# Sample tile's output projection moved into score banks and cut into quarters around the first memory tile

## Chip, cores, metric

One Trainium2 chip, one core. The time is the device time of one execution in microseconds (us), lower is better; several runs are taken and the median is given.

## What is computed (the reference, cut)

One layer of a streaming encoder for 512 prompt tokens and 64 sample tokens of width 1024. After the mixers (gated linear attention, pooling, differential attention) comes their output projection, then cross-attention to 256 memory tokens, then a mixture of 16 experts:

```python
mix = concatenate([o_gla, o_pool, o_diff.reshape(B, L, DIFF_V)], axis=-1)   # 256 + 256 + 512 columns
x = x + mix @ w_out
h = rmsnorm(x, norm_mem_g)
q = (h @ w_mem_q).reshape(B, L, MEM_HEADS, MEM_DH)                          # 4 heads of 128
s = einsum('bqhd,bkhd->bhqk', q, mk) * MEM_DH ** -0.5
p = softmax(s, axis=-1)
x = x + einsum('bqhk,bkhd->bqhd', p, mv).reshape(B, L, 512) @ w_mem_o
x = x + hier_moe(rmsnorm(x, norm_ffn_g), ...)                               # top-1 group, top-2 experts in it
```

Everything is float32. The kernel gets that precision from fast matmuls by splitting each operand into a rounded part ("high", float32r) and the rest ("low") and summing three products: high x high, high x low, low x high.

## The kernel before

**Tiles.** The tokens are five tiles: t = 0 to 3 with 128 prompt rows each, t = 4 with the 64 sample rows. For t = 4 high and low rows stand side by side in one 128-column operand, so a projection of that tile takes two matmuls for each block of 128 inputs, where the others take three; DVE then adds the two halves of the result.

**Who does what.** PE (TensorE) multiplies and transposes, ACT (ScalarE) rounds weights and transposed activations to their high parts and takes exponentials, DVE (VectorE) subtracts to get the low parts, adds projections to the residual `xw`, copies and normalises. POOL does the reciprocal roots of the norms, SP issues the loads of weights. Each engine has one written list of instructions, in order; engines wait for each other by counting semaphores.

**Banks.** PSUM has eight banks of 512 columns: `pj0`, `pj1` for projections, `tr_v`, `tr_a` for transposes, four for scores (`sc`), used in two halves of 1024 columns in turn. Three plans written by hand at the top (`projection_plan`, `transpose_plan`, `score_plan`) list every use of a bank in order, who reads it ("A" for ACT, "V" for DVE) and which bank it takes. `claim` in PE's program makes PE wait until the last user of the same bank has been read out. `high_plan` lists ACT's rounded transposes, which DVE's `low_T` waits for.

**Dense weights.** `w_in`, `w_out`, `w_mem_q`, `w_mem_o` come as 24 units of 128 x 2048, through four slots (`DRING`). Unit n takes the slot of unit n - 4, and may be loaded (SP, `dense_load`) or, for the memory query units 20 and 21, which have buffers of their own, rounded (ACT, `w_high`) when the last projection that uses unit n - 4 is done. Units 16 and 17 serve columns 0 to 511 of the mixers' projection, `w_out(0, t)`; 18 and 19 serve `w_out(1, t)`; 20 and 21 (`MQ_UNIT`) the memory queries; 22 and 23 (`MO_UNIT`) the memory output. So `w_out(0, 4)` releases 20 and 21, and `w_out(1, 4)` releases the loads of 22 and 23. `mem_q(0)` waits for DVE's `w_low` quarter by quarter (L2189), since it is the first user.

**The order around the change.** Twenty attention steps (tile, head) end with the differential attention of the sample tile. Beside its last step runs the last quarter of `w_out(1, 3)`. Then the sample's heads are normalised: ACT squares, DVE sums, POOL takes roots (L770), DVE multiplies twice into `mixd`. After that PE's list is:

```python
mixd_T(TILES - 1)          # transposes of the sample's normalised heads, bank tr_v
x1_T(0)                    # transposes of residual tile 0, halves g = 1 (tr_a), 0 (tr_v)
w_out(0, TILES - 1, 0); w_out(0, TILES - 1, 1)     # 16 matmuls, bank pj1
w_out(1, TILES - 1)                                # 16 matmuls, bank pj0
x1_T(1)
mem_q(0); mem_q_T(0); mem_scores(0)                # 24 matmuls (pj1), 4 transposes (tr_v), 8 matmuls
```

`mixd`, `mgT_pack`, `plT_pack` are the inputs of `w_out(c, 4)`: only its second half (blocks 4 to 7) needs `mixd`. Then five memory tiles follow. In tile t PE does `mem_q(t + 1)`, the transposes of the probabilities `probm` (`pm`, one half in `tr_a` for ACT, one in `tr_v` for DVE, copied at L1873), `w_mem_o(0, t - 1)`, the transposes of query t + 1 (`mem_q_T`, bank `tr_v`, copied by DVE at L1839), the memory output `mem_o(t)`, the transposes `x1_T(t + 2)`, `mem_scores(t + 1)` and `w_mem_o(1, t - 1)`. ACT evacuates `mem_q` to `rowbuf` (L985) and takes the exponentials (`exps_m`, L1279). ACT rounds units 22 and 23 before the exponentials of tile 0. DVE splits unit 22 after the row maxima of tile 0, unit 23 after those of tile 1. The first expert weights are loaded when `mem_q(4)` is done.

Lines in the profile: L2167 is the matmul helper `mm`, L2175 the transposes, L967 and L970 `w_high`, L1479 and L1450 the low parts (L1450 is any two-operand DVE operation), L944 ACT's high parts of transposes, L563 the load of units.

Of the kernel before, what the change touches and what calls it, by code (L numbers as in the profile page):

```python
# [10 lines left out]
ALU = mybir.AluOpType  # L11
# [68 lines left out]
def projection_plan():  # L80
# [11 lines left out]
    plan += [(("w_out", c, TILES - 1), "V", 1 - c) for c in range(2)]  # L92
    plan += [(("mem_q", 0), "A")]
# [17 lines left out]
def transpose_plan():  # L111
# [15 lines left out]
    plan += [(("mix_d", TILES - 1), "V", 0)] + [(("x1", 0, g), "V", g) for g in (1, 0)]  # L127
    plan += [(("x1", 1, g), "V", g) for g in range(2)] + [(("mq", 0), "V", 0)]
    for t in range(TILES):
        plan += [(("pm", t, 0), "A", 1), (("pm", t, 1), "V", 0)]  # L130
        plan += [(("mq", t + 1), "V", 0)] if t + 1 < TILES else []
        plan += [(("x1", t + 2, g), "V", g) for g in range(2)] if t + 2 < TILES else []
        plan += [(("x2", t - 2, g), "AV"[g], 1 - g) for g in range(2)] if t >= 2 else []
# [4 lines left out]
def high_plan():  # L138
# [5 lines left out]
    plan += [("mix_d", TILES - 1)] + [("x1", 0, g) for g in (1, 0)] + [("x1", 1, g) for g in range(2)]  # L144
# [26 lines left out]
def layer_program(nc, A, O):  # L171

    ctx = ExitStack()
    with ctx:
# [190 lines left out]
        pj_more = [sc[:, 1024:1536], sc[:, 1536:2048], sc[:, 0:512], sc[:, 512:1024]]  # L365
        pj_of = lambda key: (pj + pj_more)[PJ[key][3]]
# [541 lines left out]
        def _(act):  # L908
# [345 lines left out]
            def x1_high(t):  # L1254
                for g in range(2) if t else (1, 0):
# [3 lines left out]

            mixd_high(TILES - 1)  # L1260
            x1_high(0)
# [39 lines left out]
            x1_square(TILES - 1)  # L1301
            w_high(MO_UNIT)
            w_high(MO_UNIT + 1)
            act.dma_start(gffn[:, :], A["norm_ffn_g"].to_broadcast([P, D])).then_inc(gffn_in, 16)
            exps_m(0)
            for t in range(TILES):
                if t + 1 < TILES:
                    mq_out(t + 1)
                tr_out(("pm", t, 0), pmT[:, t % 2, 0:4, 0:ROWS[t]], heads_view(tr[1], 4, ROWS[t]))
                if t == TILES - 1:  # L1310
                    split_hi(0, 0, -2)
# [4 lines left out]
                if t + 1 < TILES:  # L1316
                    exps_m(t + 1)
                if t >= 2:
# [122 lines left out]
        def _(dve):  # L1441
# [324 lines left out]
            def add_rows(name, c, t, dst, src):  # L1766

                j, r, h = PJ[(name, c, t)][3], ROWS[t], slice(512 * c, 512 * c + 512)
                dve.wait_ge(pj_full, PJ[(name, c, t)][0] + 1)
                if t < 4:  # L1770
                    tt(dst[:, t, h], pj[j][:, :], src[:, t, h], ALU.add).then_inc(pj_dve, 1)
                else:
                    link(tt(dst[0:r, t, h], pj[j][0:r, :], src[0:r, t, h], ALU.add))
                    tt(dst[0:r, t, h], pj[j][r:P, :], dst[0:r, t, h], ALU.add).then_inc(pj_dve, 1)
# [32 lines left out]
            def x1_T(t):  # L1807
                for g in range(2) if t else (1, 0):
# [5 lines left out]

            mixd_low(TILES - 1)
            x1_T(0)
            w_low(MQ_UNIT)
            add_rows("w_out", 0, TILES - 1, xw, xw)
            w_low(MQ_UNIT + 1)
            x1_T(1)  # L1820
            add_rows("w_out", 1, TILES - 1, xw, xw)
# [15 lines left out]
            def q_T(t):  # L1837
                tr_wait(("mq", t))
                dve.tensor_copy(qmT[:, t % 2, :, 0:ROWS[t]], tr[0][:, :].rearrange("p (h q) -> p h q", h=MH)[:, :, 0:ROWS[t]])\  # L1839
# [22 lines left out]

            q_T(0)
            max_m(0)
            w_low(MO_UNIT)
            for t in range(TILES):
# [4 lines left out]
                   nrec[0:r, t % 2, :].unsqueeze(2).to_broadcast([r, MH, MEM]), ALU.mult).then_inc(pm_ready, 1)  # L1871
                tr_wait(("pm", t, 1))
# [18 lines left out]
                if t == 0:  # L1891
                    w_low(MO_UNIT + 1)
# [265 lines left out]
        def _(pe):  # L2158
# [10 lines left out]
            def transposes(key, blocks):  # L2169

                claim("tr", TR, TR_KEYS, key, tr_act, tr_dve)
                bank = tr[TR[key][3]]
# [5 lines left out]
            def project(key, t, hi, lo, units, w, part=None):  # L2178

                nk, j = 4 * len(units), PJ[key][3]  # L2180
                if part != 1:
                    claim("pj", PJ, PJ_KEYS, key, pj_act, pj_dve)
                out = pj_of(key)[:, 0:w]
                for k in range(nk) if part is None else range(part * nk // 2, (part + 1) * nk // 2):
# [7 lines left out]
                if part != 0:  # L2192
# [134 lines left out]
            def w_out(c, t, part=None):  # L2327
                if part != 0:
                    tr_read(pe, ("mix_d", t))
                if t == 0 and c == 0 and part != 1:  # L2330
# [91 lines left out]
            def x1_T(t):  # L2422
                pj_read(pe, ("w_out", 1, t))
                for g in range(2) if t else (1, 0):
                    transposes(("x1", t, g), [(P * k, xw_tile(t)[:, P * (4 * g + k):P * (4 * g + k) + P]) for k in range(4)])

            mixd_T(TILES - 1)
            x1_T(0)
            w_out(0, TILES - 1, 0)
            w_out(0, TILES - 1, 1)  # L2430
            w_out(1, TILES - 1)
# [8 lines left out]
            def mem_q_T(t):  # L2440
                pj_read(pe, ("mem_q", t))
# [298 lines left out]
```

## Time and profile before

| | us |
|---|---|
| median of 3 runs | 717.59 (716.68 to 719.2) |
| profiled execution, its own time | 719.38 |
| its span in the trace | 717.5 |
| PE busy | 678.9 (95%) |
| DVE busy | 522.3 (73%) |
| ACT busy | 425.2 (59%) |
| POOL busy | 141.1 (20%) |

A timeline row gives the start, the duration, the engine, the line, the operation, what it writes and reads, and how many such instructions are merged. In brackets stands how long the engine was idle before it and what ended the wait. A matmul of 512 columns shows 0.39 us, but the next one starts 0.23 us after it, because they are pipelined.

### The profile page before, as it was taken

To read this page: it belongs to the slowest core of one execution; us is meant where nothing else is said; L and a number is where in the kernel's file an instruction comes from. 1 tells how busy PE (TensorE), PEld (TensorE's weight loads), DVE (VectorE), ACT (ScalarE), POOL (GpSimd) and SP (SyncE) were. 2 spreads that over 40 slices of the span, in tenths; PEclk is the share of its full clock that TensorE was granted. 3 is DMA by queue.
4 is the path that set the end of the run, shared out by engine and by line. 5 is a ranking of instruction groups with operands and counts; after the bars stand their busy time and mean duration, and the time that the engine had idled before them with its cause. 6 is when DMAs were issued, how large, how long until landed. Compare 5 with 4: busy or idle time off the path is not lost.

```text
span 717.5 us, 9467 instructions
## 1 busy us (share of the span) xinstructions
PE 678.9 (95%) x3498; PEld 546.9 (76%) x3498; DVE 522.3 (73%) x683; ACT 425.2 (59%) x607; POOL 141.1 (20%) x160
## 2 busy tenths in 40 slices
PE   5999999999989999889999899999999999999991
PEld 4899788777667776678888678888888888888861
DVE  5346655565777674756456898899999999988983
ACT  6746633244664433453233468888888888888880
POOL 4202850021001010000002202222222222222144
PEclk9999999999999999999999999999999999999996
DMA  8724232403771000410094699999999999999773
GB/s 299 238 75 164 102 139 89 158 0 133 279 300 67 1 1 10 158 38 1 1 338 164 226 420 387 389 375 377 384 372 377 373 383 375 377 377 377 309 240 116
DMA packets 33299, 161.23 MB, mean 225 GB/s; under 512 B 6365, under 2 KB 6699, under 8 KB 18540
## 3 DMA queue, kind: packets, MB, share of 16 engines
q1 hardware_dynamic: 23680, 140.39, 50.4%
q0 software_dynamic: 5344, 10.27, 5.3%
q10 hardware_dynamic: 4236, 10.08, 3.9%
q8 instruction: 22, 0.36, 0.2%
q14 instruction: 17, 0.14, 0.1%
HBM read 149.59 MB, written 20.03 MB: 236 GB/s over the span
## 4 chain that ended last, share of the span: by engine, by line
PE 75%; DVE 13%; DMA 4%; ACT 3%; issue 2%; POOL 1%; SPq 0%; ACTq 0%; POOLq 0%; DVEq 0%
PE pj L2167 41%; PE scores L2167 17%; PE tr_v L2167 10%; DVE wl L1450 4%; PE tr_a L2175 2%; PE tr_v L2175 2%; PE scores L2579 2%; DVE w_lo L1479 2%; DMA fin<-acc_rows 2%; DMA acc_rows<-y,idx_sb 1%; PE tr_a L2608 1%; DVE hid L1450 1%; DMA raw<-in_dense 1%; POOL rs L770 1%; DMA xg<-h_rows,idx_sb 1%
## 5 line engine op out<-in xcount | busy, mean ns | idle before, releaser
L1450 DVE TENSOR_TENSOR wl<-moe_raw,wh 128x2048 fp32r<-128x2048 f32 x96 | 218.5, 2290 | 23.8 <-ACT wh L923 22.6
L923 ACT ACTIVATE wh<-moe_raw 128x2048 fp32r<-128x2048 f32 x96 | 182.3, 1920 | 32.2 <-PE scores L2167 12.0
L768 POOL TENSOR_SCALAR rs<-stat 128x1 f32<-128x1 f32 (+4 forms) x31 | 12.3, 396 | 313.6 <-DVE stat L1667 154.0
L2167 PE MATMUL pj<-w_hi,xT_hi 128*128 128x512 f32 (+2 forms) x176 | 64.4, 366 | 7.8 <-DVE w_lo L1479 7.8
L2167 PE MATMUL pj<-w_hi,xT_lo 128*128 128x512 f32 (+2 forms) x176 | 62.9, 357 | 0.0
L2167 PE MATMUL pj<-w_lo,xT_hi 128*128 128x512 f32 (+2 forms) x176 | 62.8, 357 | 0.0
L822 POOL DMA_INDIRECT acc_rows<-y,idx_sb x14 | 22.3, 1590 | 205.6 <-ACT y L1373 191.5
L2167 PE MATMUL pj<-wh,xgh 128*128 128x512 f32 x128 | 51.5, 402 | 1.1 <-issue 1.1
L2167 PE MATMUL tr_v<-wh,xgh 128*128 128x512 f32 x128 | 51.1, 399 | 0.0
L2167 PE MATMUL scores<-wh,hTh 128*128 128x512 f32 x128 | 49.9, 390 | 0.6 <-DVE hTl L1450 0.6
L1479 DVE SCALAR_TENSOR_TENSOR w_lo<-raw,pack_a,w_hi 128x512 fp32r<-128x512 f32 (+2 forms) x64 | 43.8, 745 | 9.0 <-ACT w_hi L967 9.0
L2167 PE MATMUL pj<-wh,xgl 128*128 128x512 f32 x128 | 50.0, 391 | 0.0
L2167 PE MATMUL tr_v<-wl,xgh 128*128 128x512 f32 x128 | 49.9, 390 | 0.0
L2167 PE MATMUL tr_v<-wh,xgl 128*128 128x512 f32 x128 | 49.9, 390 | 0.0
L2167 PE MATMUL scores<-wh,hTl 128*128 128x512 f32 x128 | 49.9, 390 | 0.0
L2167 PE MATMUL scores<-wl,hTh 128*128 128x512 f32 x128 | 49.8, 389 | 0.0
L2167 PE MATMUL pj<-wl,xgh 128*128 128x512 f32 x128 | 49.8, 389 | 0.0
L2167 PEld LDWEIGHTS pj<-w_hi,xT_hi 128*128 128x128 f32 x176 | 33.8, 192 | 12.7 <-POOL hide_k L744 7.8
L1161 ACT ACTIVATE prob<-scores,tiny 128x128 f32<-128x128 f32 (+4 forms) x40 | 22.4, 564 | 30.8 <-DVE tiny L1710 30.8
L967 ACT ACTIVATE w_hi<-raw,pack_a 128x512 fp32r<-128x512 f32 (+2 forms) x64 | 37.8, 662 | 3.3 <-DMA raw<-in_dense 2.5
L2167 PEld LDWEIGHTS pj<-w_hi,xT_lo 128*128 128x128 f32 x176 | 33.7, 192 | 4.7
L2167 PEld LDWEIGHTS pj<-w_lo,xT_hi 128*128 128x128 f32 x176 | 33.8, 192 | 4.3
(444 smaller groups left out, 1516.8 us busy)
## 6 DMA issues: line engine op xcount, KB each, us to landing
moe_raw<-in_w_exp_gate SPq DMA_DIRECT2D x32, 1024.0 KB, 10.0
moe_raw<-in_w_exp_up SPq DMA_DIRECT2D x32, 1024.0 KB, 11.4
moe_raw<-in_w_exp_down SPq DMA_DIRECT2D x32, 1024.0 KB, 11.8
raw<-in_dense SPq DMA_DIRECT2D x16, 1024.0 KB, 6.1
raw<-in_dense SPq DMA_DIRECT2D x8, 256.0 KB, 6.5
x_rows<-in_x_prompt SPq DMA_DIRECT2D x4, 512.0 KB, 10.7
xw<-in_x_prompt ACTq DMA_DIRECT2D x1, 2048.0 KB, 8.0
h_rows<-h ACTq DMA_DIRECT2D x4, 512.0 KB, 3.9
```

What stands on the lines that cost most here:

```text
L768: link(pool.tensor_scalar(rs[rows, n, cs], stat[rows, n, cs], EPS, None, ALU.add))
L770: pool.tensor_tensor(rs[rows, n, cs], rs[rows, n, cs], neghalf[rows, 0:width], ALU.pow)\
L822: pool.indirect_dma_start(acc_rows, bass.IndirectOffsetOnAxis(ap=idx, axis=0), y[:, b, :], None, bounds_check=TOK - 1, oob_is_err=False, c ...
L923: act.activation(wh[s4][:, :], moe_raw[n % RING][:, :], ACT.Copy).then_inc(hi_done, 1)
L967: act.activation(slot[:, w * k:w * k + w], srcs[k], ACT.Copy, scale=gains[:, GAIN_OF[name], r // P + k:r // P + k + 1]).then_inc(w_hi_done, 1)
L1161: ins = act.activation(prob[0:r, s % 2, m, 0:nk], maps(t, h, nk)[:, m, :], ACT.Exp, bias=nmax[0:r, s % 2, m:m + 1], scale=DH ** -0.5, accu ...
L1450: return dve.tensor_tensor(out, a, b, op)
L1479: dve.scalar_tensor_tensor(out=w_lo[:, n % DRING, w * k:w * k + w], in0=srcs[k], scalar=gains[:, GAIN_OF[name], r // P + k:r // P + k + 1] ...
L2167: return pe.matmul(out, lhsT, rhs, start=start, stop=stop, skip_group_check=True)
L2175: ins = pe.transpose(bank[0:n, c0:c0 + r], src, ident[0:r, 0:r])
L2579: ins = pe.transpose(px[g][:, P * k:P * k + P], xg[:, buf, P * (4 * g + k):P * (4 * g + k) + P], ident[:, :])
L2608: ins = pe.transpose(ph[:, P * k:P * k + P], hid[:, P * k:P * k + P], ident[:, :])
```

## The change

Sample tile projection: `w_out(0, 4)` and `w_out(1, 4)` write banks 4 and 5 of the list, which are columns 0 to 511 and 512 to 1023 of the scores, in place of `pj1` and `pj0`. `project` knows quarters: parts 0 and 1 are the halves as before, parts 2 and 3 the two quarters of the second half. PE's list becomes: half g = 1 of residual tile 0, first half of `w_out(0, 4)`, the sample's `mixd` transposes, first half of `w_out(1, 4)`, half g = 0 of residual tile 0 (now also `tr_a`), second half of `w_out(0, 4)`, residual tile 1, `mem_q(0)`, quarter 2 of `w_out(1, 4)`, transposes of query 0, quarter 3, scores of tile 0. The additions of the two results to `xw` on DVE move from between the splits of units 20 and 21 and the x1 splits to before and after the query copy and row maxima of tile 0. The transposes of queries 1 to 4 go to the score half that holds the scores of the tile before (columns 1024 to 1535 or 0 to 511). ACT's rounding of unit 22 moves behind its `pm` copy of tile 0, that of unit 23 behind the exponentials of tile 1, and the sample's mean square behind the exponentials of tile 0. DVE splits unit 22 after the row maxima of tile 1 and unit 23 ahead of its `pm` copy in tile 1.

```diff
         plan += beside[:1] + [(("diff_o", t), "V", 0)] + beside[1:] if t == TILES - 1 else beside + [(("diff_o", t), "V", 0)]
-    plan += [(("w_out", c, TILES - 1), "V", 1 - c) for c in range(2)]
-    plan += [(("mem_q", 0), "A")]
+    plan += [(("w_out", 0, TILES - 1), "V", 4), (("mem_q", 0), "A", 1), (("w_out", 1, TILES - 1), "V", 5)]
...
             plan += [(("mix_d", t - 1), "V", 0)] if h == 0 and t else []
-    plan += [(("mix_d", TILES - 1), "V", 0)] + [(("x1", 0, g), "V", g) for g in (1, 0)]
+    plan += [(("x1", 0, 1), "V", 1), (("mix_d", TILES - 1), "V", 0), (("x1", 0, 0), "V", 1)]
...
         plan += [(("pm", t, 0), "A", 1), (("pm", t, 1), "V", 0)]
-        plan += [(("mq", t + 1), "V", 0)] if t + 1 < TILES else []
+        plan += [(("mq", t + 1), "V", 2 + t % 2)] if t + 1 < TILES else []
...
     plan += [("mix_g", TILES - 1)] + [("mix_d", t) for t in range(TILES - 1)]
-    plan += [("mix_d", TILES - 1)] + [("x1", 0, g) for g in (1, 0)] + [("x1", 1, g) for g in range(2)]
+    plan += [("x1", 0, 1), ("mix_d", TILES - 1), ("x1", 0, 0)] + [("x1", 1, g) for g in range(2)]
...
         pj_more = [sc[:, 1024:1536], sc[:, 1536:2048], sc[:, 0:512], sc[:, 512:1024]]
+        tr_more = [sc[:, 1024:1536], sc[:, 0:512]]
...
             act.dma_start(cmv, A["cache_mem_v"][0, 0].rearrange("(b p) h d -> p b (h d)", p=P)).then_inc(cmv_in, 16)
-            def x1_high(t):
-                for g in range(2) if t else (1, 0):
+            def x1_high(t, gs=(0, 1)):
+                for g in gs:
...
+            x1_high(0, (1,))
             mixd_high(TILES - 1)
-            x1_high(0)
+            x1_high(0, (0,))
...
             mq_out(0)
-            x1_square(TILES - 1)
-            w_high(MO_UNIT)
-            w_high(MO_UNIT + 1)
...
             exps_m(0)
+            x1_square(TILES - 1)
...
                 tr_out(("pm", t, 0), pmT[:, t % 2, 0:4, 0:ROWS[t]], heads_view(tr[1], 4, ROWS[t]))
+                if t == 0:
+                    w_high(MO_UNIT)
...
                     exps_m(t + 1)
+                if t == 0:
+                    w_high(MO_UNIT + 1)
...
-                j, r, h = PJ[(name, c, t)][3], ROWS[t], slice(512 * c, 512 * c + 512)
+                bank, r, h = pj_of((name, c, t)), ROWS[t], slice(512 * c, 512 * c + 512)
...
                 if t < 4:
-                    tt(dst[:, t, h], pj[j][:, :], src[:, t, h], ALU.add).then_inc(pj_dve, 1)
+                    tt(dst[:, t, h], bank[:, :], src[:, t, h], ALU.add).then_inc(pj_dve, 1)
                 else:
-                    link(tt(dst[0:r, t, h], pj[j][0:r, :], src[0:r, t, h], ALU.add))
-                    tt(dst[0:r, t, h], pj[j][r:P, :], dst[0:r, t, h], ALU.add).then_inc(pj_dve, 1)
+                    link(tt(dst[0:r, t, h], bank[0:r, :], src[0:r, t, h], ALU.add))
+                    tt(dst[0:r, t, h], bank[r:P, :], dst[0:r, t, h], ALU.add).then_inc(pj_dve, 1)
...
-            def x1_T(t):
-                for g in range(2) if t else (1, 0):
+            def x1_T(t, gs=(0, 1)):
+                for g in gs:
...
+            x1_T(0, (1,))
             mixd_low(TILES - 1)
-            x1_T(0)
+            x1_T(0, (0,))
             w_low(MQ_UNIT)
-            add_rows("w_out", 0, TILES - 1, xw, xw)
...
             x1_T(1)
-            add_rows("w_out", 1, TILES - 1, xw, xw)
...
                 tr_wait(("mq", t))
-                dve.tensor_copy(qmT[:, t % 2, :, 0:ROWS[t]], tr[0][:, :].rearrange("p (h q) -> p h q", h=MH)[:, :, 0:ROWS[t]])\
+                bank = (tr + tr_more)[TR[("mq", t)][3]]
+                dve.tensor_copy(qmT[:, t % 2, :, 0:ROWS[t]], bank[:, :].rearrange("p (h q) -> p h q", h=MH)[:, :, 0:ROWS[t]])\
...
+            add_rows("w_out", 0, TILES - 1, xw, xw)
...
             max_m(0)
-            w_low(MO_UNIT)
+            add_rows("w_out", 1, TILES - 1, xw, xw)
...
                    nrec[0:r, t % 2, :].unsqueeze(2).to_broadcast([r, MH, MEM]), ALU.mult).then_inc(pm_ready, 1)
+                if t == 1:
+                    w_low(MO_UNIT + 1)
...
                 if t == 0:
-                    w_low(MO_UNIT + 1)
+                    w_low(MO_UNIT)
...
                 claim("tr", TR, TR_KEYS, key, tr_act, tr_dve)
-                bank = tr[TR[key][3]]
+                bank = (tr + tr_more)[TR[key][3]]
...
                 nk, j = 4 * len(units), PJ[key][3]
-                if part != 1:
+                ks_of = {0: range(nk // 2), 1: range(nk // 2, nk), 2: range(nk // 2, 3 * nk // 4), 3: range(3 * nk // 4, nk)}
+                if part in (None, 0):
...
                 out = pj_of(key)[:, 0:w]
-                for k in range(nk) if part is None else range(part * nk // 2, (part + 1) * nk // 2):
+                for k in range(nk) if part is None else ks_of[part]:
...
                         ins = mm(out, lo(k), w_hi[:, n % DRING, c], False, k == nk - 1)
-                if part != 0:
+                if part not in (0, 2):
...
                     tr_read(pe, ("mix_d", t))
-                if t == 0 and c == 0 and part != 1:
+                if t == 0 and c == 0 and part in (None, 0):
...
                     mixd_T(t - 1)
-            def x1_T(t):
+            def x1_T(t, gs=(0, 1)):
                 pj_read(pe, ("w_out", 1, t))
-                for g in range(2) if t else (1, 0):
+                for g in gs:
...
+            x1_T(0, (1,))
+            sc_read(pe, ("diff", 4, HEADS - 1, 0))
+            w_out(0, TILES - 1, 0)
             mixd_T(TILES - 1)
-            x1_T(0)
-            w_out(0, TILES - 1, 0)
+            w_out(1, TILES - 1, 0)
+            x1_T(0, (0,))
             w_out(0, TILES - 1, 1)
-            w_out(1, TILES - 1)
...
                 pj_read(pe, ("mem_q", t))
+                if t:
+                    sc_read(pe, ("mem", t - 1))
...
                     pe.wait_ge(cmk_in, 16)
+                if t == 1:
+                    pj_read(pe, ("w_out", 1, TILES - 1))
...
             mem_q(0)
+            w_out(1, TILES - 1, 2)
             mem_q_T(0)
+            w_out(1, TILES - 1, 3)
```

## Rows read from the trace of the kernel before

**Rows 1.** The page, part 1: busy time of each engine over the whole span.
```profile
PE 678.9 (95%) x3498; PEld 546.9 (76%) x3498; DVE 522.3 (73%) x683; ACT 425.2 (59%) x607; POOL 141.1 (20%) x160
```

**Rows 2.** Busy time by stretch: PE, PEld, DVE, ACT, POOL, clock, DMA share, GB/s.
```profile
330.00:412.00 82.00, 79.37 (x490) 66.24 (x489) 52.33 (x100) 30.88 (x64) 9.91 (x15) 1.00 0.44 157
412.00:660.00 248.00, 246.91 (x1166) 202.06 (x1165) 226.75 (x177) 197.42 (x163) 50.99 (x26) 1.00 1.00 383
```

**Rows 3.** The chain that ended last: start us, us, what.
```profile
295.98 2.74 DVE w_lo L1479 x4
```

**Rows 4.** Timeline of PE, 289 to 318 us: start, us, line, what, [idle before <-releaser].
```profile
289.29 0.46 PE L2175 MATMUL tr_v<-ident,mixd 64*128 64x64 f32 x4 [1.38 <-DVE mixd L1450]
...
290.81 0.66 PE L2175 MATMUL tr_v<-ident,xw 128*128 128x128 f32 x4 [0.48 <-DVE mdT_hi L1450]
291.23 0.47 PE L2167 MATMUL pj<-w_hi,mgT_pack 128*128 128x512 f32 x1
...
294.73 0.39 PE L2167 MATMUL pj<-w_lo,mdT_hi 128*128 128x512 f32 x1
...
300.30 0.47 PE L2167 MATMUL pj<-w_hi,x1T_hi 128*128 128x512 f32 x1 [0.67 <-DVE xw L1450]
...
306.86 0.66 PE L2175 MATMUL tr_v<-ident,rowbuf 128*128 128x128 f32 x4 [0.84 <-ACT rowbuf L985]
308.30 1.99 PE L2167 MATMUL scores<-mkT,qmT 128*128 128x256 f32 x8 [0.79 <-DVE qmT L1839]
...
315.63 0.60 PE L2175 MATMUL tr_a<-ident,probm 128*128 128x128 f32 x4
...
317.54 0.63 PE L2175 MATMUL tr_v<-ident,rowbuf 128*128 128x128 f32 x4 [0.88 <-DVE pmT L1873]
...
318.00 1.95 PE L2167 MATMUL pj<-pmT,mv 128*128 128x128 f32 x16
```

**Rows 5.** Timeline of ACT, 295 to 320 us.
```profile
295.22 2.57 ACT L967 ACTIVATE w_hi<-mq_raw,pack_a 128x512 fp32r<-128x512 f32 x4 [2.08 <-PE pj L2167]
...
307.75 3.70 ACT L970 ACTIVATE w_hi<-raw 128x2048 fp32r<-128x2048 f32 x2
311.80 0.47 ACT L1279 ACTIVATE probm<-scores,tiny 128x256 f32<-128x256 f32 x1 [0.35 <-DVE tiny L1847]
...
315.88 0.69 ACT L985 ACTIVATE rowbuf<-pj,rs 128x512 f32<-128x512 f32 x1 [2.16 <-PE pj L2167]
316.47 0.59 ACT L989 ACTIVATE pmT<-tr_a 128x512 f32<-128x512 f32 x1
319.99 0.60 ACT L944 ACTIVATE omT_hi<-pj 128x512 fp32r<-128x512 f32 x1 [2.93 <-PE pj L2167]
```

**Rows 6.** Timeline of DVE, 302 to 317 us.
```profile
302.72 0.69 DVE L1450 TENSOR_TENSOR x1T_lo<-tr_v,x1T_hi 128x512 fp32r<-128x512 f32 x1
...
303.92 1.40 DVE L1450 TENSOR_TENSOR xw<-pj,xw 64x512 f32<-64x512 f32 x2
307.55 0.69 DVE L1839 COPY qmT<-tr_v 128x512 f32<-128x512 f32 x1 [2.23 <-PE tr_v L2175]
...
311.67 2.29 DVE L1450 TENSOR_TENSOR w_lo<-raw,w_hi 128x2048 fp32r<-128x2048 f32 x1
...
316.70 0.69 DVE L1873 COPY pmT<-tr_v 128x512 f32<-128x512 f32 x1 [1.39 <-PE tr_v L2175]
```

**Rows 7.** The page, part 6: DMA issues, KB each, median us to landing.
```profile
moe_raw<-in_w_exp_down SPq DMA_DIRECT2D x32, 1024.0 KB, 11.8
raw<-in_dense SPq DMA_DIRECT2D x16, 1024.0 KB, 6.1
```

**Rows 8.** Busy time by stretch, columns as in rows 2.
```profile
184.00:185.00 1.00, 1.00 (x7) 0.68 (x6) 0.71 (x4) 0.22 (x1) 0.00 (x0) 0.50 0.91 352
288.00:291.00 3.00, 1.23 (x10) 0.93 (x11) 2.23 (x4) 0.98 (x2) 0.00 (x0) 1.00 0.52 201
```

**Rows 9.** Timeline of PE at 186 us.
```profile
186.30 0.63 PE L2167 MATMUL pj<-w_lo,memT_hi 128*128 128x512 f32 x1
```

## The prediction, made before the changed kernel was run

> **What bounds the kernel now.** The page's busy line comes first: TensorE (PE) 95%, VectorE (DVE) 73%, ScalarE (ACT) 59% of the span [rows 1]. The windows come second: from 412 to 660 us, the experts, PE is busy 246.91 of 248 us, and from 330 to 412 us 79.37 of 82 us [rows 2]. The change touches neither stretch but for the banks of four small transposes, so the question is what PE waits for between 284 and 330 us, and whether a lead won there is kept. The chain of waits puts DVE's splits of the memory query weights into the chain at 295.98 us [rows 3]. The timeline of PE then gives its stalls in brackets [rows 4]:
> - 1.38 us at 289.29: transposes of the sample's mixd wait for the norm of the last attention tile;
> - 0.48 us at 290.81: bank tr_v is held until DVE has read them;
> - 0.67 us at 300.30: memory query projection mem_q(0) waits for bank pj1, which DVE frees by adding w_out(0,4);
> - 0.84 us at 306.86 and 0.79 us at 308.30: the evacuation of mem_q(0) by ACT, then of its transposes by DVE;
> - 0.88 us at 317.54: transposes of query 1 wait for tr_v, which DVE is still copying to pmT.
>
> Together 5.04 us. Matmuls of 512 columns show 0.39 us each but start 0.23 us apart, so in starts each stall is some 0.16 us longer, about 6 us. That is the most there is to win.
>
> **The change part by part.** No matmul, transpose, evacuation or DMA is added or removed; the sum is one of stalls and order.
>
> *Around the last norm.* PE is free for a new start at 287.75 us (287.91, the end before the 1.38 us stall, less 0.16). Four transposes take 0.42 us (290.81 to 291.23), eight matmuls 1.92 us (half of the 16 between 291.23 and 294.96, one start after 294.73, with a slightly longer first), the small mixd transposes 0.39 us [rows 4]. The new order is four x1 transposes, 8 matmuls of w_out(0,4), mixd transposes, 8 of w_out(1,4), four x1 transposes, 8 of w_out(0,4): 0.43 + 1.92 + 0.39 + 1.92 + 0.43 + 1.92 = 7.0, to 294.76 us. PE reaches the mixd transposes at 290.1, after mixd is there (289.29), so 1.38 and 0.48 us vanish, their place being taken by half of w_out(1,4). DVE's x1 split, now queued ahead of the mixd split, is over before mixd is transposed (290.5), and PE does not need mdT before 292.9; it delays nothing. The last matmul of w_out(0,4) ends at 294.92 instead of 295.12.
>
> *The query weights.* That end releases ACT's rounding of units 20 and 21. It starts at 295.02 instead of 295.22 [rows 5]: this chain, not PE, now sets mem_q(0). PE does the x1 transposes of tile 1 until 295.6, then waits for the first quarter. ACT does a quarter in 0.64 us (2.57 for four), DVE in 0.685 us (2.74 for four), starting 0.76 us behind ACT [rows 3, 5]. With the two sample adds (1.40 us [rows 6]) gone from between the units, DVE runs all eight quarters from 295.78: the last is there at 295.78 + 8 x 0.685 = 301.26. PE needs 0.68 us for a quarter's three matmuls, so it keeps step; the last three end at 302.2 us. Before, mem_q(0) ended 0.84 us ahead of the transposes, at 306.02 [rows 4]. Lead: **3.8 us**. The bounds: were PE not paced but merely started at the first quarter (296.5) it would end at 302.0; were the pace a quarter slower, 0.85 us, the last split would come at 302.6 and the lead be 2.5 us. I take 3.8, since these are the same instructions with the same neighbours as in the rows.
>
> *Two quarters of w_out(1,4).* Four matmuls each, 0.91 us, run while ACT evacuates mem_q(0) (0.69 us, starting 0.10 us after its end as at 295.22 [rows 5]) and while DVE copies the transposes. The first ends at 302.97, the query rows are there at 303.0, so the transposes start at 303.06 (306.86 before). Their end is 303.72; DVE has by then done two x1 splits (302.72 to 303.92 before, 301.26 to 302.4 now) and the sample add it now has first (1.40 us, to 303.8), so the copy starts within 0.1 us of its input. Scores 0.75 us after it [rows 4, 6]: 304.5 instead of 308.30. The 0.84 and 0.79 us have become 0.1 and 0.15 us. Lead still 3.8 us. The first exponential came 3.5 us after the scores began (311.80), so now at 308.0; four at 0.47 us last until 309.9. The second add stands on DVE between the row maximum and the normalisation that waits for them (308.0 to 309.4): free. So is ACT's sample square behind them, of 1,024 elements where a rounding of 2,048 takes 1.85 us [rows 5]: it starts at 309.9 and the next evacuation is due at 312.1.
>
> *Query transposes in score halves.* From the scores PE reaches the probability transposes 7.33 us later (308.30 to 315.63), at 311.83. Transposes of query 1 no longer wait for pmT but only for ACT's rows (315.88 + 0.69, 0.94 us after the probability transposes began): 312.83. The memory output behind them still needs pmT, which DVE has 1.76 us after they began; it starts at 1.91 us instead of 2.37 us [rows 4 to 6], so **0.46 us**, not 0.88. From 330 to 412 us PE idles 2.6 us in all [rows 2], none of it in front of query transposes, so the other three in score banks win nothing; and their banks have long been read, so they lose nothing.
>
> *The output units.* SP may load units 22 and 23 only when w_out(1,4) ends, now 304.6 instead of 298.6. A load takes 6.1 us [rows 7]; both should land by 312. ACT's first rounding (1.85 us) stands behind its copy to pmT (316.47 + 0.59 before, 313.3 now) and ahead of the memory output's (319.99 before, 315.7 now); DVE's splits (2.29 us each) go to 319.7 to 322.0 and, ahead of pmT in tile 1, 323.6 to 325.9 [rows 5, 6]. That copy of pmT slips 0.9 us there, but PE asks for it 3 us after its transposes, with 1.4 us left. The projection that uses unit 22 is at 324.7. Cost nothing; uncovered, the late units cost what they exceed these margins by.
>
> **Sum.** 3.8 + 0.46 = 4.25 us. The experts' first loads are released by mem_q(4), which moves with the rest, and the gather, router and experts follow PE's chain, so the lead reaches the end. The profiled execution took 719.38 us (span 717.5 and 1.88 us around it), 0.25% above the median of 717.59; I expect 715.1 for it and, for the median, 717.59 - 4.25 = **713.3 us**.
>
> **The rivals.**
> *Loads late (no change).* The output units' loads are released 6 us later, and ACT's rounding stands in its queue ahead of the rounding of the first memory output. Beside traffic, 1 MB takes 11.8 us to land in the row of the expert weights [rows 7]: 304.7 + 11.8 = 316.5. ACT must start by 313.85 to be done at 315.7, so 2.65 us are lost and 1.6 won: 716.0 us. Against it: the queues are empty there except for 0.5 MB of gains.
> *Split pace (smaller gain).* The 0.85 us pace above: lead 2.5 + 0.46 = 3.0 us, 714.6 us.
> *PE's clock (slower).* From 184 to 185 us, where PE has just done transposes and short matmuls, the granted clock is 0.50, the 1.2 GHz level, and 512-column matmuls take 0.63 us in place of 0.39, so start 0.43 us apart if the overlap stays as it is; the last such row is at 186.30 us [rows 8, 9]. In 2.6 us six are done and each costs 0.2 to 0.24 us: about 1.5 us lost per episode. Memory tiles have such stretches (from 315.63 us [rows 4]). If the new query transposes, queued with fewer waits between other small work, brought this on in each of the five tiles, 7.5 us would be lost against 4.25 won: 720.8 us. It decides from three tiles on. Against it: at 288 to 291 us PE is busy 1.23 of 3 us, mostly with transposes, at a clock of 1.00 [rows 8], and the change puts matmuls of full width into just such holes.
> The Trainium skill, "TensorE: Matmul & The Clock Gate", Part 4, says that PE transposes do not count as busy for the clock as matmuls do. By that rule long runs of them would bring on the slower case; the trace agrees at 184 us and contradicts it as a sufficient cause at 288 to 291 us.
>
> **How the numbers follow.** 0.3% is 2.15 us, about what a measurement of this kernel can tell from no change. Forecast 0.79, split pace 0.09 (both faster), late loads 0.08 (same), clock 0.04 (slower): faster 0.88, same 0.08, slower 0.04. The range goes from the full 5.0 us of stalls (712.6) to a lead of 2.5 us (715.1), and 0.5 to 0.7 us further at each end since the runs before spread from 716.68 to 719.2: 711.9 to 715.8.
>
> **What would show it.** In the new profile: no wait for mixd or mdT_hi; a wait of PE of some 0.9 us for w_lo at the start of mem_q(0), which ends near 302.2; waits of 0.1 to 0.2 us at rowbuf and qmT; one of about 0.4 us for pmT, now at the memory output; first scores at 304.5; raw landing before 313. The reasoning is wrong if w_out(0,4) ends later than 295.1, if mem_q(0) ends after 303.5, if a new wait for w_lo or omT_hi stands at 314 to 330, or if a window there has a clock under 1.

## The result, and the profile after

The changed kernel takes 714.05 us (median of 9 runs, 713.06 to 715.75), the kernel before 719.2 us (median of 9, 716.68 to 721.26): ratio 0.9929, 95% interval 0.9913 to 0.9944. The forecast was 713.3 us in a range of 711.9 to 715.8. The profiled execution took 713.37 us (span 711.5) instead of 719.38 (717.5); 715.1 was forecast for it. (A slip ahead of the prediction: the wait of `mem_q(0)` for the split quarters is at L2187, not L2189.)

**The order around the norm.** Timeline of PE in the changed kernel; helper lines have moved, L2173 is the matmul, L2181 the transpose:

```profile
282.92 0.50 PE L2173 MATMUL pj<-w_hi,mdT_hi 128*128 128x512 f32 x1
...
285.78 0.60 PE L2181 MATMUL tr_a<-ident,xw 128*128 128x128 f32 x4
286.13 0.47 PE L2173 MATMUL scores<-w_hi,mgT_pack 128*128 128x512 f32 x1
...
288.15 0.46 PE L2181 MATMUL tr_v<-ident,mixd 64*128 64x64 f32 x4
288.53 0.50 PE L2173 MATMUL scores<-w_hi,mgT_pack 128*128 128x512 f32 x1
...
290.46 0.60 PE L2181 MATMUL tr_a<-ident,xw 128*128 128x128 f32 x4
290.81 0.48 PE L2173 MATMUL scores<-w_hi,mdT_hi 128*128 128x512 f32 x1
...
294.67 0.47 PE L2173 MATMUL pj<-w_hi,x1T_hi 128*128 128x512 f32 x1 [0.88 <-DVE w_lo L1482]
```

No transpose has a bracket any more: the waits of 1.38 and 0.48 us [rows 4] are gone, and one of 0.88 us for the split weights stands in front of mem_q(0). To compare times, take the first row as an anchor: it begins the last twelve matmuls of w_out(1,3), ahead of everything that was changed, and stood at 284.90 us before.

**The query and the first memory tile**, the same timeline further on:

```profile
300.23 0.39 PE L2173 MATMUL scores<-w_hi,mdT_hi 128*128 128x512 f32 x1
...
301.23 0.66 PE L2181 MATMUL tr_v<-ident,rowbuf 128*128 128x128 f32 x4
301.64 0.47 PE L2173 MATMUL scores<-w_hi,mdT_hi 128*128 128x512 f32 x1
...
302.67 1.99 PE L2173 MATMUL scores<-mkT,qmT 128*128 128x256 f32 x8
309.96 0.60 PE L2181 MATMUL tr_a<-ident,probm 128*128 128x128 f32 x4
...
310.96 0.66 PE L2181 MATMUL scores<-ident,rowbuf 128*128 128x128 f32 x4
311.87 2.02 PE L2173 MATMUL pj<-pmT,mv 128*128 128x128 f32 x16 [0.25 <-DVE pmT L1879]
314.60 1.89 PE L2173 MATMUL scores<-mkT,qmT 128*128 128x256 f32 x8
```

The waits for rowbuf and qmT [rows 4] have gone below what a bracket shows, and pmT is now waited for 0.25 us by the memory output in place of 0.88 us by the query transposes, which write a score bank.

The splits that PE waits for at the start of mem_q(0), on DVE in the timeline of the changed kernel (w_lo of units 20 and 21, now with nothing between; then the first sample add and the first query copy):

```profile
293.77 2.74 DVE L1482 SCALAR_TENSOR_TENSOR w_lo<-mq_raw,pack_a,w_hi 128x512 fp32r<-128x512 f32 x4 [1.29 <-ACT w_hi L967]
296.43 1.40 DVE L1482 SCALAR_TENSOR_TENSOR w_lo<-mq_raw1a,pack_a,w_hi 128x512 fp32r<-128x512 f32 x2
297.76 1.41 DVE L1482 SCALAR_TENSOR_TENSOR w_lo<-mq_raw1b,pack_a,w_hi 128x512 fp32r<-128x512 f32 x2
...
300.28 1.40 DVE L1453 TENSOR_TENSOR xw<-scores,xw 64x512 f32<-64x512 f32 x2
301.92 0.69 DVE L1842 COPY qmT<-tr_v 128x512 f32<-128x512 f32 x1 [0.24 <-PE tr_v L2181]
```

Seen from the anchor, in us (before, forecast, after; the gathered rows are PE's first transposes for the experts):

| | before | forecast | changed |
|---|---|---|---|
| last row of mem_q(0) ends | 21.12 | 17.3 | 17.47 |
| first scores start | 23.40 | 19.6 | 19.75 |
| second scores start | 35.76 | 31.5 | 31.68 |
| gathered rows | 124.11 | 119.9 | 120.04 |

The lead is 3.65 us at the first scores and **4.07 us** at the gathered rows. It is kept, as the stretches behind have the same shape as in [rows 2] (windows of the changed kernel):

```profile
330.00:405.00 75.00, 72.47 (x445) 59.95 (x443) 48.84 (x95) 29.32 (x61) 9.03 (x15) 1.00 0.46 166
405.00:655.00 250.00, 248.69 (x1173) 203.36 (x1174) 228.72 (x181) 197.44 (x163) 51.87 (x27) 1.00 1.00 383
```

But the medians differ by 5.15 us and the spans by 6.0 us, and the anchor itself is 1.98 us earlier (282.92 instead of 284.90). Nothing ahead of the anchor was changed. That surplus is the open question of the second half of the experiments.

### The profile page after: what moved, and what is told of

It is laid out like the page before. It is cut to its first block, busy times and chain, and to the rows that moved or that the text cites. A ratio compares the mean times of both kernels' runs of the same rounds, so it can differ in the third digit from the quotient of the medians.

```text
span 711.5 us, 9467 instructions
## 1 busy us (share of the span) xinstructions
PE 676.8 (95%) x3498; PEld 545.4 (77%) x3498; DVE 521.7 (73%) x683; ACT 425.5 (60%) x607; POOL 141.4 (20%) x160
## 4 chain that ended last, share of the span: by engine, by line
PE 76%; DVE 12%; DMA 4%; ACT 3%; issue 3%; POOL 1%; ACTq 0%; POOLq 0%; DVEq 0%; SPq 0%
PE pj L2173 41%; PE scores L2173 18%; PE tr_v L2173 10%; DVE wl L1453 4%; PE tr_a L2181 2%; PE scores L2594 2%; PE tr_v L2181 1%; DVE w_lo L1482 1%; DMA acc_rows<-y,idx_sb 1%; DMA xs_next<-acc_rows,idx_sb 1%; PE tr_a L2623 1%; DVE hid L1453 1%; DMA raw<-in_dense 1%; DMA xg<-h_rows,idx_sb 1%; DVE w_lo L1453 1%
## 5 line engine op out<-in xcount | busy, mean ns | idle before, releaser
L2173 PE MATMUL pj<-w_hi,xT_hi 128*128 128x512 f32 (+2 forms) x176 | 64.4, 366 | 7.8 <-DVE w_lo L1482 7.8
L2173 PE MATMUL pj<-w_hi,xT_lo 128*128 128x512 f32 (+2 forms) x176 | 62.7, 357 | 0.0
L2173 PE MATMUL pj<-w_lo,xT_hi 128*128 128x512 f32 (+2 forms) x176 | 62.6, 355 | 0.0
L2173 PE MATMUL pj<-wh,xgh 128*128 128x512 f32 x128 | 51.5, 402 | 1.1 <-issue 1.1
L2173 PE MATMUL tr_v<-wh,xgh 128*128 128x512 f32 x128 | 51.1, 399 | 0.0
L2173 PE MATMUL scores<-wh,hTh 128*128 128x512 f32 x128 | 49.9, 390 | 0.6 <-DVE hTl L1453 0.6
L2173 PE MATMUL pj<-wh,xgl 128*128 128x512 f32 x128 | 50.0, 391 | 0.0
L2173 PE MATMUL tr_v<-wl,xgh 128*128 128x512 f32 x128 | 49.9, 390 | 0.0
L2173 PE MATMUL tr_v<-wh,xgl 128*128 128x512 f32 x128 | 49.9, 390 | 0.0
L2173 PE MATMUL scores<-wh,hTl 128*128 128x512 f32 x128 | 49.9, 390 | 0.0
L2173 PE MATMUL scores<-wl,hTh 128*128 128x512 f32 x128 | 49.8, 389 | 0.0
L2173 PE MATMUL pj<-wl,xgh 128*128 128x512 f32 x128 | 49.8, 389 | 0.0
L2173 PEld LDWEIGHTS pj<-w_hi,xT_hi 128*128 128x128 f32 x176 | 33.7, 191 | 12.6 <-POOL hide_k L744 7.8
L2173 PEld LDWEIGHTS pj<-w_hi,xT_lo 128*128 128x128 f32 x176 | 33.6, 191 | 4.7
L2173 PEld LDWEIGHTS pj<-w_lo,xT_hi 128*128 128x128 f32 x176 | 33.8, 192 | 4.3
## 6 DMA issues: line engine op xcount, KB each, us to landing
moe_raw<-in_w_exp_up SPq DMA_DIRECT2D x32, 1024.0 KB, 11.6
```

Of the source, the lines that this page charges most:

```text
L2173: return pe.matmul(out, lhsT, rhs, start=start, stop=stop, skip_group_check=True)
```

## The experiments

Each is built on the kernel named; all times from the anchor are from its one profiled execution, the ratios against runs of the kernel before.

**The queries back in tr_v**

```diff
-        plan += [(("mq", t + 1), "V", 2 + t % 2)] if t + 1 < TILES else []
+        plan += [(("mq", t + 1), "V", 0)] if t + 1 < TILES else []
```

> The changed kernel with the transposes of queries 1 to 4 back in bank tr_v, nothing else. Counted from the start of the last twelve matmuls of w_out(1,3) (the anchor), the changed kernel has its first scores at 19.75 us, its second at 31.68, the transposes of the gathered rows at 120.04; the kernel before had 23.40, 35.76 and 124.11. My account (the query banks give 0.46 us, because the memory output behind them waits for pmT anyway): first scores as in the changed kernel, second at 32.1, gathered rows at 120.5. Rival (the bank wait of 0.88 us is won in full): second scores at 32.6. Rival (the banks matter in all tiles): gathered rows at 122 or later.

Measured: first scores 19.74, second 32.08, gathered rows 120.55; ratio 0.9928 (0.9907 to 0.9948). The 0.88 us wait is back, and yet only 0.4 to 0.5 us are lost. The wait for the bank hid the wait of the next instruction for the same copy.

**The half of w_out(1,4) whole, ahead of mem_q(0)**

```diff
             w_out(0, TILES - 1, 1)
+            w_out(1, TILES - 1, 1)
             x1_T(1)
...
             mem_q(0)
-            w_out(1, TILES - 1, 2)
             mem_q_T(0)
-            w_out(1, TILES - 1, 3)
```

(with the two entries of `projection_plan` in the new order)

> The changed kernel with the whole second half of w_out(1,4) ahead of the x1 transposes of tile 1, no quarters inside the memory query. My account: the half fills the wait for the first split quarter (0.88 us), runs 0.8 us over it, and the two evacuation waits of 0.8 us each come back empty: mem_q(0) ends 0.75 us later, first scores at 20.5 us after the anchor in place of 19.75, the whole run 0.75 us slower than the changed kernel. Rival (the quarters in the two waits are the main gain): both waits are lost outright, first scores at 21.5 us.

Measured: first scores 20.44, gathered rows 120.85; ratio 0.9927 (0.9911 to 0.9942). The wait for w_lo is gone, those of 0.8 us for rowbuf and qmT are back. The quarters in the two evacuation waits are worth 0.7 to 0.8 us, not the 1.6 us that they fill, since the same eight matmuls could have stood in the wait for the splits.

**The old order around the norm**

```diff
-            x1_T(0, (1,))
+            mixd_T(TILES - 1)
+            x1_T(0, (1, 0))
             sc_read(pe, ("diff", 4, HEADS - 1, 0))
             w_out(0, TILES - 1, 0)
-            mixd_T(TILES - 1)
-            w_out(1, TILES - 1, 0)
-            x1_T(0, (0,))
             w_out(0, TILES - 1, 1)
+            w_out(1, TILES - 1, 0)
```

(with the plans and the lists of ACT and DVE in the same order)

> The changed kernel with the order of before around the norm (mixd transposes, both halves of x1(0), w_out(0,4) whole, then the first half of w_out(1,4)); banks, quarters and later adds stay. My account: the waits for mixd (1.38 us) and mdT (0.48 us) return, but they partly replace the wait for the first split quarter, since the weight splits start only 0.2 us later: mem_q(0) becomes bound by PE again and ends about 0.95 us later; first scores at 20.7 us after the anchor. Rival (what fills the norm's wait is gained in full): 1.9 us or more, first scores at 21.6 us.

Measured: first scores 20.68, gathered rows 120.97; ratio 0.9955 (0.9935 to 0.9974). The interval from the anchor is 0.93 us longer, as expected; the runs show more, 0.9955 against 0.9929 of the time before, which is 1.9 us (medians 716.8 and 714.05 us, taken at different times). Waits in this kernel's trace:

```profile
PE tr_v L2179 <- DVE mixd L1452: 1.4, 1, 1.4
...
PE tr_v L2179 <- DVE mdT_hi L1452: 0.5, 1, 0.5
PE pj L2171 <- DVE pmT L1877: 0.3, 1, 0.3
```

**DVE's first sample add between the splits**

```diff
             w_low(MQ_UNIT)
+            add_rows("w_out", 0, TILES - 1, xw, xw)
             w_low(MQ_UNIT + 1)
             x1_T(1)
...
-            add_rows("w_out", 0, TILES - 1, xw, xw)
             q_T(0)
```

> The changed kernel with DVE's first sample add (1.40 us) back between the splits of units 20 and 21. My account (mem_q(0) is paced by DVE's splits): the second unit is 1.35 us late, a new wait for w_lo stands inside mem_q(0), first scores at 21.1 us after the anchor, the run 1.35 us slower than the changed kernel. Rival (mem_q(0) is bound by PE, DVE has slack): first scores within 0.2 us of 19.75.

Measured: first scores 20.97, gathered rows 121.16; ratio 0.9944 (0.9925 to 0.9963). PE now waits for w_lo twice, 1.8 us in all. So mem_q(0) hangs on DVE's splits with little to spare, and the moved add is worth 1.2 us of the lead at the first scores, 1.1 of the 4.07 at the gathered rows. In the changed kernel itself PE waits only for the first of the splits.

**ACT's rounding of the output units early again**

```diff
+            w_high(MO_UNIT)
+            w_high(MO_UNIT + 1)
             exps_m(0)
```

(and the two later calls taken out)

> The changed kernel with ACT's rounding of output units 22 and 23 back ahead of the exponentials of tile 0, as in the kernel before; nothing else. The loads of these units are released only when w_out(1,4) ends (302.84 us in the changed kernel's trace) and take 5.9 us. My account (the later splits are what makes the late end of w_out(1,4) affordable): first scores stay at 19.75 us after the anchor, ACT waits for the load, the exponentials come some 6.1 us late, PE waits as long for the normalised probabilities; second scores at 37.8 instead of 31.68, gathered rows at 126. Rival (the moved splits are a side matter, ACT has slack there): second scores within 1 us of 31.68.

Measured: first scores 19.77, second 40.8, gathered rows 129.13; ratio 1.0065 (1.0046 to 1.0083), slower than before. ACT's timeline in this kernel:

```profile
307.96 1.92 ACT L970 ACTIVATE w_hi<-raw 128x2048 fp32r<-128x2048 f32 x1 [7.10 <-DMA raw<-in_dense]
311.43 1.91 ACT L970 ACTIVATE w_hi<-raw 128x2048 fp32r<-128x2048 f32 x1 [1.55 <-DMA raw<-in_dense]
313.24 0.46 ACT L1280 ACTIVATE probm<-scores,tiny 128x256 f32<-128x256 f32 x1
```

The exponentials begin at 313.24 instead of 306.17 us, seen from the two anchors 7.4 us late where 6.1 were expected: the second unit landed only at 311.4. PE stands still for 6.8 us, with nothing at all from 310 to 316 us, and its clock is at 0.50 to 0.54 in every window of 1 us from 315 to 322 us. PE's transposes of the probabilities come 7.05 us later than in the changed kernel, the second scores 9.12 us later, so the low clock adds some 2 us. The move of the roundings brings nothing itself, but the rest can't do without it.

**The kernel before with the banks alone**

```diff
-    plan += [(("w_out", c, TILES - 1), "V", 1 - c) for c in range(2)]
-    plan += [(("mem_q", 0), "A")]
+    plan += [(("w_out", c, TILES - 1), "V", 4 + c) for c in range(2)]
+    plan += [(("mem_q", 0), "A", 1)]
```

(with the change's bank argument in `add_rows` and its two waits for the score banks)

> The kernel before with w_out(0,4) and w_out(1,4) in the score banks and nothing else changed. My account: only the wait of mem_q(0) for bank pj1 (0.67 us, 0.8 us in starts) goes; first scores at 22.6 us after the anchor instead of 23.40, gathered rows at 123.3 instead of 124.11; the weight splits, though as late as before, are not waited for. Rival (the banks alone carry the gain): first scores at 20 to 21 us.

Measured: first scores **24.06** instead of 22.6, gathered rows 124.72; ratio 0.9990 (0.9972 to 1.0008). The wait for pj1 is gone, and still the scores come later than before. The windows of this trace show why:

```profile
288.00:289.00 1.00, 0.53 (x5) 0.29 (x4) 0.42 (x1) 0.86 (x2) 0.00 (x0) 0.98 0.00 0
289.00:290.00 1.00, 1.00 (x5) 1.00 (x6) 0.69 (x1) 0.12 (x1) 0.00 (x0) 0.50 0.00 0
290.00:291.00 1.00, 1.00 (x4) 0.81 (x3) 0.19 (x1) 0.89 (x2) 0.00 (x0) 0.50 0.00 0
291.00:292.00 1.00, 1.00 (x3) 0.72 (x3) 0.51 (x1) 0.75 (x2) 0.10 (x1) 0.50 0.00 0
```

The granted clock (third number from the right) is at 0.50, the 1.2 GHz level, from 289 to 292 us, behind the waits at the norm. The right comparison is therefore with a profile of the kernel before that fell at the same place. There is one below, with first scores at 24.86 and gathered rows at 124.11 + 1.46 = 125.57 us: against it the banks alone give 0.80 us at the scores, as expected, and 0.85 us at the gathered rows. No profile of the banks alone without the fall was taken.

**Every wait filled**

```diff
             w_out(0, TILES - 1, 1)
+            w_out(1, TILES - 1, 2)
             x1_T(1)
...
             mem_q(0)
-            w_out(1, TILES - 1, 2)
+            w_out(1, TILES - 1, 3)
             mem_q_T(0)
-            w_out(1, TILES - 1, 3)
+            mem_q(1, 4)        # its first three matmuls
             mem_scores(0)
```

(the later call of `mem_q(1)` takes the rest)

> The changed kernel with the first quarter of the second half of w_out(1,4) moved into the wait for the split weights (ahead of the x1 transposes of tile 1), the second into the wait for the evacuation of mem_q(0), and the first three matmuls of mem_q(1) into the wait for the copied query transposes. My account: no wait but those of some 0.1 us is left before the first scores, which stay at 19.75 us after the anchor since the weight splits and the two evacuations set them; mem_q(1) ends 0.68 us earlier, but the probabilities are ready only 6.9 us after the first scores: second scores at 31.3 instead of 31.68, gathered rows at 119.7 instead of 120.04, too little for the run times. Rival (PE is the bound here): second scores at 31.0. If mem_q(0) is held up by the quarter before it: first scores later than 19.8.

Measured: first scores 19.72, second 31.38, gathered rows 119.78; 713.38 us (median of 7), ratio 0.9932 (0.9909 to 0.9956). The lead over the changed kernel is 0.26 us in the trace and can't be told by the runs. PE's timeline shows where it stops:

```profile
309.20 0.66 PE L2181 MATMUL tr_a<-ident,probm 128*128 128x128 f32 x4 [0.17 <-DVE probm L1453]
...
311.17 2.02 PE L2173 MATMUL pj<-pmT,mv 128*128 128x128 f32 x16 [0.44 <-DVE pmT L1879]
```

The softmax of the first tile is the next bound.

**The changed kernel again**

No edit.

> The changed kernel itself, once more, for the spread. My account: the change is worth 4.07 us from the anchor on (gathered rows at 120.04 instead of 124.11 us), and what a run has beyond that comes ahead of the anchor, where both kernels are the same: in the first profile of before the granted clock is 0.62 from 184 to 188 us and the anchor at 284.9, in that of the changed kernel 1.00 and 282.92. So in this profile 120.0 again whatever the anchor, and an anchor near 284.9 if the clock between 183 and 188 us is under 1, else near 283. Rival (the change itself is worth the 5 to 6 us by which medians and spans differ): anchor at 283 and a clock of 1.00 there every time.

Measured: first scores 19.73, gathered rows 120.06, anchor 283.17, clock 1.00 between 184 and 188 us; 714.02 us (median of 9), ratio 0.9939 (0.9917 to 0.9961). This profile alone can't tell the two accounts apart, as the anchor near 283 us and the full clock are also what the rival says. Against the rival speak two kernels above that are the changed one up to the norm and beyond: with the queries back in tr_v the anchor is at 285.12 us, with the half ahead of mem_q(0) at 284.87 us, both with a clock of 0.50 from 184 to 187 us.

**The norm's wait filled with unused matmuls**, in the kernel before

```diff
+            sc_read(pe, ("diff", 4, HEADS - 1, 0))
+            for k in range(6):
+                mm(sc[:, 0:512], mgT_pack[:, k % 2, :], w_hi[:, WO_UNIT % DRING, 512 * (k % 4):512 * (k % 4) + 512], True, True)
             mixd_T(TILES - 1)
```

> The kernel before with six added matmuls of 512 columns into a free score bank, read by nobody, between the last matmul of w_out(1,3) and the transposes of mixd; their results are not used. They take 1.37 us of PE and lie inside its wait for mixd (1.54 us from start to start). Question: the medians of before and of the changed kernel differ by 5.1 us and the traces from the anchor on by 4.07; the profile of the kernel with the banks alone showed the granted clock at 0.50 from 289 to 292 us, right behind the waits at the norm. My account (in part of the runs of before the clock falls there, in the changed kernel the wait is full of matmuls and it does not): first scores at 23.4 us after the anchor as in the kernel before, no clock under 1 at 286 to 294 us, and a median about 0.5 to 1 us below that of before with mean clocks of 0.992 and above in more of the runs. Rival (the fall at 289 us is chance and as common in both kernels, or only the one at 184 us counts): the median of before, 719.5 us, within 0.4 us.

Measured: first scores 23.42, gathered rows 124.02; 717.84 us (median of 12 runs), ratio 0.9980 (0.9965 to 0.9994). The clock stays at 1.00 at the norm:

```profile
286.00:288.00 2.00, 1.72 (x11) 0.95 (x10) 1.50 (x3) 0.60 (x2) 0.00 (x0) 1.00 0.37 143
```

More work, unchanged order, the same interval in the trace, and some 1.4 us (0.4 to 2.5) off the runs.

**The kernel before, twice more, and the filled one once more**

> The kernel before once more, for its clock. First scores at 23.40 us after the anchor, gathered rows at 124.1, unless the clock falls between anchor and scores: then about 1.5 us more on both, with a clock of 0.5 in the windows from 286 to 294 us. By my account some runs of this kernel have that and none of the changed kernel; one profile shows it with a chance of one in three or so.

Measured: first scores 24.86, gathered rows 125.57; ratio 0.9991 (0.9977 to 1.0005), as it must be. Windows of this trace, from 286 us:

```profile
286.00:288.00 2.00, 0.62 (x6) 0.32 (x4) 1.78 (x3) 0.00 (x0) 0.15 (x1) 1.00 1.01 400
288.00:290.00 2.00, 1.53 (x11) 1.26 (x9) 1.19 (x3) 0.98 (x2) 0.00 (x0) 0.71 0.08 30
290.00:292.00 2.00, 2.00 (x7) 1.61 (x6) 0.81 (x2) 1.63 (x3) 0.00 (x0) 0.50 0.00 0
```

and its PE timeline, where matmuls take 0.63 us and start 0.43 us apart as in [rows 9]:

```profile
287.64 0.46 PE L2175 MATMUL tr_v<-ident,mixd 64*128 64x64 f32 x4 [1.38 <-DVE mixd L1450]
...
290.50 0.63 PE L2167 MATMUL pj<-w_lo,mgT_pack 128*128 128x512 f32 x1
290.93 0.63 PE L2167 MATMUL pj<-w_hi,mgT_pack 128*128 128x512 f32 x1
```

> A further profile of the kernel before, for the same question: either 23.4 us from anchor to first scores at a clock of 1.00, or some 24.9 us with a clock of 0.5 for some 3 us between 286 and 294 us.

Measured (one execution, 720.71 us): first scores 24.91, clock 0.51 from 290 to 292 us: the same again. This execution has one more fall, at 0.50 from 412 to 414 us, behind two waits of 0.90 and 1.02 us with the eight transposes of the gathered rows between them. Of the fourteen profiles only this one and that with the roundings early have it there.

> A further profile of the kernel before with the six added unused matmuls at the norm: by my account 23.4 us from anchor to first scores and a clock of 1.00 from 286 to 294 us. A fall of the clock there would speak against the account.

Measured (one execution, 719.74 us): first scores 23.41, clock 1.00 at the norm; here it had fallen at 184 us instead (anchor 285.25).

## Why the prediction was right

**The lead from the anchor on** was forecast at 4.25 us and is 4.07. *Around the norm:* PE's walk of 7.0 us from 287.75 came out as 7.0 (285.78 to 292.76), the waits for mixd and mdT gone, and the splits began 0.2 us earlier against the anchor, as said. *The query weights:* eight quarters on DVE took 5.40 us (293.77 to 299.17) where 5.48 were reckoned. But mem_q(0) ended 1.22 us after the last of them, not 0.94. PE began it 11.75 us after the anchor (11.6 reckoned) and took 5.72 us for its 24 matmuls, as it had before (300.30 to 306.02 us). So behind the first quarter PE's own pace set the end, where the prediction let the splits set it. The lead is 3.65 instead of 3.8 us, the largest miss of any term. *Quarters:* no wait left at rowbuf and qmT (0.1 to 0.15 forecast). *Query transposes:* 0.43 instead of 0.46 us, and the run with them back in tr_v lost 0.4 to 0.5. *Output units:* ACT rounded them without waiting, at cost nothing; the condition on that, that they stand late in ACT's queue, was the hard one: with them early the kernel is slower than before.

**The rivals.** Late loads did not happen: the first rounding ran at 311.28 us at once. Slower splits did not happen. The clock rival had the mechanism right and its sign wrong for this change. It said that light stretches of PE can bring the clock down, at some 1.5 us each, and feared that for the changed order. In the runs it is the old order that has the light stretch which matters, and the memory tiles, where it was feared, stayed at 1.00 in every profile but the one with a standstill of 6.8 us.

**What was missing** is that gain. The step of the argument that failed is the sentence that took the clock of 1.00 at 288 to 291 us in one profile [rows 8] for the rule. Thirteen further profiles say otherwise. Of the five kernels or executions with the norm's wait open (before three times, the old order, the banks alone) three fell at the norm and the other two at 184 us, each exactly once ahead of the scores. Of the nine with the wait filled (by the change or by unused matmuls) none fell at the norm, three at 184 us, and six had no fall ahead of the first scores. A fall costs 1.46 and 1.51 us at the norm (24.86 and 24.91 against 23.40) and 1.55 us at 184 us (from the scores at 183.65 to those at 188.93 us before, 183.23 to 186.96 after). One fall in every profile against one in three makes about 1.0 us, and 4.07 + 1.0 = 5.1 us, which is the difference of the medians. That filling the norm's wait alone gives 1.4 us (0.4 to 2.5) in the runs, with the interval in the trace unchanged, supports it. The counts are small, and why a fall at 184 us and one at the norm never came together was not tried.

The timed executions carry this further, since nearly all have their mean clock on record. In the profiles it is 0.989 or 0.990 with one fall and 0.991 to 0.993 with none (every profile is also at 0.50 for its last 10 to 13 us, whatever the kernel). The executions of all rounds together, with their mean time in us:

| | mean clock 0.990 or less | 0.992 or more | 0.991 |
|---|---|---|---|
| before, 76 executions | 49 (720.1) | 19 (717.9) | 8 |
| changed, 18 | 4 (716.1) | 13 (714.0) | 1 |
| norm filled with unused matmuls, 13 | 4 (719.7) | 9 (717.8) | 0 |

At a like clock the change is worth 4.0 us (95% interval by resampling, 3.2 to 4.6) and 3.9 us (3.3 to 4.4), in line with the 4.07 of the traces, and the unused matmuls 0.4 and 0.1 us. The remainder is that a low mean clock is rarer: 64% of the executions before, 22% of the changed kernel. At 2.1 to 2.2 us between the classes that makes 0.9 us. Two things stay open. A quarter of the executions of the kernel before look like those without a fall, so a fall in every one, as in the five profiles, is not the rule. And the classes lie further apart than one fall costs; where the clock fell in these executions is not on record.

The rest of the 1.98 us at the anchor, some 0.4 us, was there before 183 us and is spread between executions: without a fall at 184 us the anchors lie from 282.30 to 283.58 us, with one from 284.73 to 285.25 us. So the profiled execution came out 1.7 us under its forecast of 715.1 us for a reason of its own: the profile of before, from which that was reckoned, had the fall at 184 us and this one had not.

The forecast of 713.3 us lies only 0.75 us below the measured 714.05 by luck, because two differences nearly cancel: the base was 717.59 us by three runs and is 719.2 us by nine (1.6 us more), and the gain was forecast at 4.25 us and is 5.15 (0.9 us more).

The Trainium skill, "TensorE: Matmul & The Clock Gate", Part 4, says that transposes do not count for the clock as matmuls do. The traces agree in so far as the falls come behind stretches of transposes and waits (PE busy 0.62 of 2 us from 286 to 288 us above) and stay away when six or eight full matmuls stand in the same place; that transposes alone would do it no run here shows. Nor are they needed: with the roundings early the clock fell behind a standstill alone.

## What to carry to other kernels

A wait that is filled is worth only what the next chain leaves: six waits of 5.0 us together gave 4.1, since the weight splits took over, and each part undone cost 0.4 to 1.2 us in the traces. When a result is finished later, everything that its end releases (here the load of the next weights) has to move down the queues of the other engines too, or the gain turns into a loss of several microseconds. And a wait between transposes should be judged by several profiles: besides its own length it can cost the clock of the matmuls behind it, in some executions and not in others.

## What was not expected of the hardware

The granted clock fell to 0.50 behind 1.4 and 0.5 us of waiting with eight short transposes between, in three of five profiled executions, and in none of nine with full matmuls in the same wait; each fall cost about 1.5 us. With the roundings early, both 1 MB loads were issued from 302.53 us on, and ACT could begin on the first at 307.96 and on the second at 311.43, that is 5.4 and 8.9 us later. Counted from its own issue each, the first took 5.3 and the second 8.4 us to land (5.9 and 8.4 us in the changed kernel): the median of 6.1 us [rows 7] hides the second of a pair.
